# Lower parts of the mixers' split weights: made by GpSimd instead of VectorE

## The reference

```python
p = y @ w_in                       # 512x1024 @ 1024x4104
mq, mk, mv, mo, mif, hq, hf, hi, hg = split(p)
q, k = silu(causal_dwconv([mq, mk]))               # 4 taps
hm = mlstm(q, k, mv, gates)        # 4 heads of 128, scores with decay weights
ho = hgrn2(silu(hq), 1 - fgate, hi, log(fgate))    # 4 heads of 128
out = [norm(hm) * sigmoid(mo), norm(ho) * silu(hg)] @ w_out
```

## Time and profile before

| | |
|---|---|
| median of 3 runs | 2471.71 us (2471.34 to 2474.63) |
| the profiled execution: its time, its span | 2473.02 us, 2471.3 us |
| PE, DVE, ACT, POOL busy | 98%, 60%, 43%, 5% of the span |
| granted PE clock over the span | 0.996 |
| the mixer with its slots | about 470 to 727 us of the span |

### The profile page before, as it was taken

One profiled execution on the slowest core, in us unless ns is written; L12 is line 12 of the kernel. 1 busy time (PEld: TensorE's weight loads), 2 busy tenths in 40 slices (PEclk: granted clock), 3 DMA queues, 4 the chain that ended last, 5 costly groups with the idle time before them and its releaser, 6 DMA issues.

```text
span 2471.3 us, 29408 instructions
## 1 busy us (share of the span) xinstructions
PE 2426.0 (98%) x11466; PEld 1963.8 (79%) x11466; DVE 1484.5 (60%) x2462; ACT 1051.5 (43%) x1703; POOL 119.1 (5%) x188
## 2 busy tenths in 40 slices
PE   7999999999999999999999999999999999999999
PEld 5878888877878888887887788888788767888886
DVE  4886535777667333346664866633867768555337
ACT  4343334545556333233444423233656654323333
POOL 0000211001010000000000000000011100000000
PEclk9999999999999999999999999999999999999999
DMA  9555566544233233222322233224243313323231
GB/s 371 180 181 193 188 223 118 88 82 118 71 115 121 89 102 102 93 95 87 109 71 76 86 102 103 87 93 134 88 137 103 118 35 102 103 86 101 94 128 68
DMA packets 240217, 286.88 MB, mean 116 GB/s; under 512 B 9640, under 2 KB 223272, under 8 KB 239824
## 3 DMA queue, kind: packets, MB, share of 16 engines
q1 hardware_dynamic: 222752, 230.21, 30.3%
q0 software_dynamic: 15552, 51.62, 6.5%
q10 hardware_dynamic: 1776, 3.18, 0.3%
HBM read 267.12 MB, written 18.09 MB: 115 GB/s over the span
## 4 chain that ended last, share of the span: by engine, by line
PE 83%; DVE 10%; ACT 4%; issue 2%; DMA 1%; ACTq 0%; DVEq 0%; POOL 0%
PE G L2350 69%; PE X L2350 2%; DVE acc L1536 2%; DVE wl L1547 2%; PE G L2897 1%; DVE yl L1585 1%; DVE h L1660 1%; PE G L2427 1%; PE G L2423 1%; ACT yh L960 1%; PE G L2424 1%; PE G L2837 1%; PE X L2632 1%; PE X L2804 1%; PE X L2878 1%
## 5 line engine op out<-in xcount | busy, mean ns | idle before, releaser
L1547 DVE TENSOR_TENSOR wl<-raw,wh 128x1024 fp32r<-128x1024 f32 (+1 forms) x394 | 472.2, 1203 | 627.2 <-ACT wh L889 626.9
L889 ACT ACTIVATE wh<-raw 128x1024 fp32r<-128x1024 f32 (+1 forms) x394 | 406.2, 1037 | 717.0 <-PE G L2350 695.2
L2350 PE MATMUL G<-yh,wh 128*128 128x512 f32 x1704 | 680.4, 399 | 11.7 <-DVE yl L1565 5.2
L2350 PE MATMUL G<-yl,wh 128*128 128x512 f32 x1704 | 665.1, 390 | 0.0
L2350 PE MATMUL G<-yh,wl 128*128 128x512 f32 x1704 | 664.8, 390 | 0.0
L2350 PEld LDWEIGHTS G<-yh,wh 128*128 128x128 f32 x1704 | 320.4, 188 | 85.3 <-issue 9.8
L2350 PEld LDWEIGHTS G<-yl,wh 128*128 128x128 f32 x1704 | 320.3, 188 | 68.5
L2350 PEld LDWEIGHTS G<-yh,wl 128*128 128x128 f32 x1704 | 320.6, 188 | 65.8 <-issue 2.2
L2350 PE MATMUL G<-hidh,wh 128*128 128x512 f32 x704 | 274.0, 389 | 0.0
L2350 PE MATMUL G<-hidl,wh 128*128 128x512 f32 x704 | 273.9, 389 | 0.0
L2350 PE MATMUL G<-hidh,wl 128*128 128x512 f32 x704 | 273.9, 389 | 0.0
(11 more groups left out here) (437 smaller groups left out, 3234.8 us busy)
## 6 DMA issues: line engine op xcount, KB each, us to landing
raw<-in_ffn_w_in SPq DMA_DIRECT2D x44, 1024.0 KB, 4.9
raw<-in_ffn_w_gate SPq DMA_DIRECT2D x22, 1024.0 KB, 5.2
raw<-in_ffn_w_up SPq DMA_DIRECT2D x22, 1024.0 KB, 5.3
ada_c<-in_ada_w POOLq DMA_DIRECT2D x20, 1024.0 KB, 5.7
raw<-in_ffn_w_down SPq DMA_DIRECT2D x16, 1024.0 KB, 4.9
raw<-in_w_in SPq DMA_DIRECT2D x16, 1024.0 KB, 9.8
raw<-in_ffn_w_out SPq DMA_DIRECT2D x16, 1024.0 KB, 4.9
ada_z<-in_ada_w SPq DMA_DIRECT2D x14, 1024.0 KB, 10.8
```

The source lines that it names most:

```text
L889: nc.scalar.activation(place(wh), src, ACT.Copy).then_inc(hi, 1)
L1547: nc.vector.tensor_tensor(place(wl), src, f32(place(wh)), ALU.subtract).then_inc(lo, 1)
L2350: ins = nc.tensor.matmul(bank, a, b, start=first and i == 0, stop=last and i == 2)
```

## The change

For the blocks that follow block 6, `split_lo` goes from DVE's queue to POOL's: 28 splits, weight blocks 10 to 37 counted from the mixer's first. 27 of them are 128x1024, and one, of the small gate block, is 128x1x4. The last four belong to the output projection `mixo`. POOL gets them in the same slots, behind the `affine_select` of the slot and ahead of its `add_rows`. In the slots without `affine_select`, which are the 40 H slots and some others, POOL has only the splits. Each still waits for `hi`; the first also waits until DVE's last `lo`. After the mixer DVE takes the splits up again, behind a wait until POOL's are done.

```diff
+            def split_lo(hh):                       # on POOL
+                pool.wait_ge(hi, hh + 1)
+                if hh == BB["mix"] + 10:
+                    pool.wait_ge(lo, hh)
+                src, place = half_parts(hh)
+                nc.gpsimd.tensor_tensor(place(wl), src, f32(place(wh)), ALU.subtract).then_inc(lo, 1)
...
-                    for n in range(NH * TT):
-                        x, j = divmod(n, TT)
-                        pool.wait_ge(wexp, n + 1)
...
+                    for s, (z, kind, x, j) in enumerate(SLOTS):
+                        score = kind == "M" and j < TT
+                        if score:
+                            n = TT * x + j
+                            pool.wait_ge(wexp, n + 1)
+                            w = C2[:, n % 2, 0:P]
+                            nc.gpsimd.affine_select(out=w, in_=w, ...).then_inc(wdiag, 1)
+                        if s:
+                            for b, of, _, t, _ in blocks_behind(s - 1):
+                                splits_behind(b, of, t)
+                        if score:
+                            for i in ((), (), (1,), (2,))[j]:
+                                add_rows(x, i)
...
-                    if s:                           # DVE's loop over the slots
-                        for b, kind, _, t, _ in blocks_behind(s - 1):
-                            splits_behind(b, kind, t)
...
             mix()
+            dve.wait_ge(lo, BB["mixo"] + 4)
             product("mixo", 3, yo_mix)
```

More of the change, by code:

```diff
@@ L772, in add_rows, with splits_behind @@
                     .then_inc(att_summed, 1)
+            def split_lo(hh):
[4 more added lines that the diff above has]
+                nc.gpsimd.tensor_tensor(place(wl), src, f32(place(wh)), ALU.subtract).then_inc(lo, 1)
+            def splits_behind(b, kind, t):
+                if kind not in ("v", "hi"):
+                    split_lo(b + 4)
+                elif t:
+                    split_lo(b + 3)
+                    split_lo(b + 4)
+                if kind == "if":
+                    split_lo(b + 5)
             def load_halves():
@@ L827, in _ @@
                         nc.gpsimd.memset(f32(rows[:, :]), 0.0).then_inc(memset_done, 1)
-                    for n in range(NH * TT):
-                        x, j = divmod(n, TT)
-                        pool.wait_ge(wexp, n + 1)
[L831 to L836, removed]
+                    for s, (z, kind, x, j) in enumerate(SLOTS):
[4 more added lines that the diff above has]
+                            w = C2[:, n % 2, 0:P]
+                            nc.gpsimd.affine_select(out=w, in_=w, compare_op=ALU.is_ge, fill=0.0, base=0,
+                                                    pattern=[[1, P]], channel_multiplier=-1).then_inc(wdiag, 1)
+                        if s:
[4 more added lines that the diff above has]
+                                add_rows(x, i)
+                        if score and n == 2 * TT - 1:
                             pool.wait_ge(rows_out, 16)
@@ L1791, in block @@
                             .then_inc(gfree[BANK[g]], 1)
[L1793 to L1800, removed]
                 def level_sums(z, x):
```

## The result

The changed kernel takes **2480.9 us** (median of 7 runs, 2479.3 to 2482.0) where the kernel before takes 2473.7 us beside it (7 runs, 2471.3 to 2474.6). The ratio is 1.0031, 95% interval [1.0021, 1.0041]: by the medians 7.2 us slower, by the interval between 5.2 and 10.1. The profiled execution took 2480.05 us with a span of 2478.3 us, 7.0 us more than before.

The account below looks back on a forecast made before the run. PE, busy for 98% of the span, was taken as the bound, so only its waits count. Terms 4.1 + 1.4 + 1.15 + 0.3 - 1.2 - 0.45 = +5.3 us on 2471.7 gave 2477.0 us, range 2468.5 to 2483.

Parts of the forecast that it names:

- convolutions, slots 2, 4, 10, 12: H slots 2, 4, 10, 12: POOL's split holds DVE's level_mul; PE waits 1.0, 1.05, 1.0, 0.35 us.
- slot 18: If POOL gets the inputs ahead of DVE's level_mul, PE's level comes late: +1.4 us; if DVE wins, nothing.
- slot 25, forget gates: POOL's split holds DVE's forget gates ahead of the scores: +1.15 us; -1.1 if they are not blocked.
- slots 51 to 53, `mo` copy: POOL's affine_select, split and addition alternate with DVE's gates: +0.3 us at the copy, in place of a gain.
- slot 55, scores of M3: POOL starts behind two of DVE's gates, so these scores come 1.2 us earlier: -1.2 us.
- small: In the mixer, a PE wait of 0.4 us goes, with 0.1 of unmarked idle time: -0.45 us.
- Slots 36 to 43: DVE is blocked as often but ahead of PE, 3.1 us in hand: 0; uncovered, 1.0 us for each of seven.
- DVE's busy time: In the mixer it should not fall by 32 us but stay or grow, since blocked time counts as busy.
- B: Blocked instructions cost PE nothing, so DVE's relief in the mixer gains 3.0 us: 2468.7 us; chance 0.10.
- A: Engines take turns, but slots 18 and 25 fall the other way: 0 to +4 us, 2472 to 2476; chance 0.27.
- C: DVE becomes the mixer's bound: 32 us if standing hits PE at all 27 splits, 16 at half; chance 0.13.
- D: POOL's queue: affine_select behind a split delays scores in M slots; 0 to +2 us, inside the range.

Follow-up runs that it names:

- e1: The changed kernel with each moved subtraction replaced by two POOL memsets, which write but read nothing: 2471.05 us, ratio 0.9991 to the kernel before.
- e2: The changed kernel with splits 10 to 25 back on DVE, 26 to 37 on POOL: 2472.69 us, ratio 0.9997 to the kernel before.
- e5: The changed kernel with splits 26 to 37 back on DVE, 10 to 25 on POOL: 2480.95 us, ratio 1.0033 to the kernel before.
- e6: The kernel before with only split 22 (slot 25) moved to POOL: 2474.12 us, ratio 1.0005 to the kernel before.
- e12: e10 executed again unchanged: the kernel before with slot 25's last gate instruction done three times; single execution 2471.51 us.
- e10: The kernel before, all splits on DVE, with slot 25's last gate instruction done three times; single execution 2473.10 us.
- e4: The changed kernel with each 128x1024 split done in four POOL instructions of 128x256: 2479.18 us, ratio 1.0024 to the kernel before.

## Why the prediction was right, and where its sizes were off

**The mechanism and the sign were right.** The time lies in the range, 3.9 us above the forecast; 2.0 of these are that the kernel before took 2473.7 us beside it and not 2471.7. What made it slower is what the prediction named: DVE and POOL take turns, and only where DVE was just ahead of PE does that cost. e1 shows it for `level_mul` by taking the reads away, e2 and e5 by the places, e6 for slot 25. That the sum comes so near is in part luck. Without the lower clock, which it didn't have, the measured terms add up to 5.5 us against 5.3, because the convolutions cost 1.2 less than reckoned and the `mo` copy and the small terms 1.5 more. In "SBUF — State Buffer", section "Who interferes with whom", the Trainium skill has a VectorE instruction with two SBUF inputs and a GpSimd instruction that reads SBUF exclude each other for the whole instruction. This trace agrees, with `level_mul` ending 0.29 us behind POOL.

| step | predicted, us | measured, us |
|---|---|---|
| convolutions, slots 2, 4, 10, 12 | +3.4 | +2.2 |
| convolution, slot 31 | +0.7 | +0.8 |
| slot 18 | +1.4 | +1.5 |
| slot 25, forget gates | +1.15 | +0.9 |
| slots 51 to 53, `mo` copy | +0.3 | +0.8 |
| slot 55, scores of M3 | -1.2 | -1.2 |
| small | -0.45 | +0.5 |
| lower clock, two stretches | not seen | +3.1 |
| sum | +5.3 | +8.6 |

A measured term is how much the start of the same PE instruction moved from before to after across the step: +2.2 us behind slot 12 (528.88 against 526.69), +3.7 behind slot 18 (574.49 against 570.75), +4.7 at slot 25 (585.65 against 580.98), +6.1 behind the first stretch of lower clock, +5.9 at 609.41 (603.47), +6.7 at 686.30 (679.59), +7.55 at the `mo` copy (702.00 against 694.45), +8.0 at the scores of M3 (711.10 against 703.12, with 1.24 of wait less), +8.66 at the end. The first stretch is worth 1.4 us, the second 1.7 (+7.55 to +9.2, just ahead of the scores of M3).

- *The convolutions.* The first three of the four gave 1.1, 0.2 and 0.5 us and the fourth 0.4, where I had 1.0, 1.05, 1.0 and 0.35. "In slot 4 the distances are the same" is true of DVE, whose `level_mul` takes 1.44 us there too. But PE had a small wait of 0.2 to 0.4 us at these places already or just behind them (489.35, 517.52 and 522.56 before), and where a step began with PE's own delay the hold was partly hidden. This is the step that failed: each stall was reckoned alone, "none of it comes back", while a stall of PE is slack for DVE at the next place. In slot 4 PE was 1.10 us later than before when it came to `pair`, and DVE's `level_mul` started only 0.27 us later (488.81 against 488.54): in between DVE no longer had the split that took 1.27 us of its time at 482.31.
- *The `mo` copy.* Here the term was too small, 0.3 against 0.8. I had seen the alternation, but not that three DVE gates meet three POOL instructions.
- *Slots 36 to 43.* The cover holds, there and in the H slots behind them. `level_mul` takes up to 2.64 us (at 667.61), and PE has no marked wait for DVE between 612 and 686.
- *DVE's busy time.* "Should not fall by 32 us but stay or grow": that was wrong. Over the mixer's own length it fell from 199.9 to 190.2 us. Splits of 32 us went and some 20 came back as standing, since most splits have nothing beside them that they could hold for long.
- *The clock.* This is the term that the sum lacked. The earlier trace rows had 1.00, and waits of 2.1 and 1.7 us without a loss behind them, and I took it that a wait costs its own length. In 11 of the 14 cases counted under e12, the longer waits cost 1.1 to 1.7 us more (2.6 behind the longest).

The rivals: B, relief wins, fell in the kernel as it is. e1, where relief is nearly alone, has 3.3 us in the mixer against B's 3.0, but not by B's terms: places up to 550 us gave 1.8 where B had 0.4, slot 25 gave 0.5 instead of 1.1 (its gate is held by a memset), and the `mo` copy came 0.4 later instead of earlier; only M3's 1.2 is as reckoned. A, the coin falls the other way, fell, in both executions of the changed kernel. In slot 18 it was neither of the two cases: DVE's first half went ahead of POOL, POOL got in before the second half, and it cost 1.5 us all the same. C, DVE becomes the bound, fell: DVE is busy for 64% of the stage. D cost part of the 0.82 us at the `mo` copy.

The mixer's +8.6 and the span's +7.0 differ by what lies behind the mixer, 1720.2 us after and 1721.8 before. In the changed kernel's second execution that part took 1723.6 us, so nothing is to be read from it.

## What to carry to other kernels

Moving an elementwise operation to an idle engine is priced by what the engines share, not by the idle engine's free time. List which instructions beside it use the same memory, and among them those on which the bounding engine waits within the moved instruction's duration. Here 13 of 28 splits could go without a cost that can be measured, and all 28 cost 7 us. Compare such kernels over a stretch between two fixed instructions: it repeated to 0.1 us in the changed kernel, whose two spans differ by 1.8; where it differed, by 1.1 us between e10 and e12, the granted clock says why.

## What the runs showed of the hardware

- **One input can be enough.** A DVE instruction with a single input in SBUF and its output there (`hk` from `hf`, 128x512) is held by GpSimd's subtraction as those with two are: 2.49 us instead of 0.43. The prediction had no row for this. Other forms with one input were not tried.
- **GpSimd's memset doesn't hold `level_mul`, but it holds that gate instruction.** 54 memsets of 128x1024, 0.97 us each, left `level_mul` at 418 ns. The last gate instruction, the only one that met a memset for long, took 1.13 us instead of 0.43 and ended 0.28 us behind the memset. That is one case.
- **The turns are taken between instructions.** Four subtractions of a quarter let DVE in behind the first (0.84 us against 2.49), at a price of 3.2 instead of 2.4 us for the whole.
- **A wait of PE of about 2 us may cost more than itself.** Behind 11 of 14 waits of 1.9 to 3.3 us (slot 25) and 2.5 to 2.9 us (the `mo` copy), and once behind 1.2 us (e4), the granted clock fell to the lower level for 3 to 4 us, 1.1 to 1.7 us lost each time, and for about 7 us with 2.6 us lost behind the longest. Behind 8 waits of 1.7 to 2.1 us for the `mo` copy it never did. One and the same kernel had it in one execution and not in another.
